# Output projection of a decoder layer: the sample rows multiply the raw fp32 weights in four column groups instead of split weights in a full-width tile

## The reference

```python
def _merge(x, attn, pool, ga, gb, ma, mb, gate, w_a_proj, w_b_proj, w_out):
    a = (attn * jax.nn.silu(ga)) @ w_a_proj
    bb = (pool * jax.nn.silu(gb)) @ w_b_proj
    m = jax.nn.sigmoid(ma) * a + jax.nn.sigmoid(mb) * bb
    return x + gate[:, None, :] * (m @ w_out)
```

## Time and profile before

| | us |
|---|---|
| median of 3 runs (lowest, highest) | 2156.23 (2155.46, 2157.18) |
| profiled execution, its own time | 2155.81 |
| span from the first to the last instruction | 2154.0 |
| TensorE matmuls busy in the span | 2027.2 (94%) |
| VectorE, GpSimd, ScalarE busy | 1252.5, 756.8, 493.6 |
| output projection | 1921.6 to the end |

### The profile page before, as it was taken

The page is one execution under the profiler, slowest core; times in us unless marked ns, Lnnn a source line. Parts: engine busy times, 40 slices in busy tenths (PEclk is TensorE's granted clock), DMA queues, the critical chain, the costliest instruction groups (busy, mean ns, idle before and its releaser), DMA issues.

```text
span 2154.0 us, 35342 instructions
## 1 busy us (share of the span) xinstructions
PE 2027.2 (94%) x15138; PEld 1850.8 (86%) x15138; DVE 1252.5 (58%) x1510; ACT 493.6 (23%) x621; POOL 756.8 (35%) x254
## 2 busy tenths in 40 slices
PE   4699999998999999999999999999988899989997
PEld 1289999988898988898999999999877898877776
DVE  2356666576787878885556777779533721133223
ACT  3222222342212222222112211112211311122222
POOL 0043333552233323233333444444444343323331
PEclk7799999999999999999999999999999999999999
DMA  9942223534232322233332233333466564633222
GB/s 343 353 141 79 78 79 92 156 105 140 71 83 68 82 74 78 72 87 107 80 98 70 69 97 99 96 97 105 136 171 167 167 196 142 201 111 125 86 100 102
DMA packets 325058, 258.68 MB, mean 120 GB/s; under 512 B 6587, under 2 KB 275063, under 8 KB 323655
## 3 DMA queue, kind: packets, MB, share of 16 engines
q1 hardware_dynamic: 312943, 228.10, 36.1%
q0 software_dynamic: 5120, 16.77, 2.6%
q10 hardware_dynamic: 6912, 12.59, 1.9%
HBM read 246.43 MB, written 11.48 MB: 120 GB/s over the span
## 4 chain that ended last, share of the span: by engine, by line
PE 79%; DVE 11%; DMA 5%; issue 2%; ACT 1%; SPq 0%; POOL 0%; DVEq 0%; ACTq 0%; POOLq 0%
PE acc L1358 59%; PE ps L1746 8%; DMA ring<-in_w_ada 4%; DVE ebuf L1060 2%; DVE qiT L935 2%; PE ps L1426 1%; PE acc L1746 1%; DVE ebuf L1061 1%; PE ps L1542 1%; PE ps L1552 1%; DVE idx L1056 1%; DVE scoreS L1058 1%; PE ps L1532 1%; PE ps L1683 1%; DVE misc L1053 1%
## 5 line engine op out<-in xcount | busy, mean ns | idle before, releaser
L463 POOL TENSOR_TENSOR wlo<-raw,whi 128x2048 fp32r<-128x2048 f32 (+1 forms) x170 | 681.8, 4015 | 1085.0 <-ACT whi L560 1084.6
L1358 PE MATMUL acc<-act_hi,whi 128*128 128x260 f32 x3904 | 814.3, 290 | 11.3 <-DVE act_lo L1188 6.2
L1358 PE MATMUL acc<-act_hi,wlo 128*128 128x260 f32 x3904 | 788.2, 283 | 0.0
L1358 PE MATMUL acc<-act_lo,whi 128*128 128x260 f32 x3904 | 787.6, 283 | 0.0
L1358 PEld LDWEIGHTS acc<-act_hi,whi 128*128 128x128 f32 x3904 | 607.7, 190 | 48.7 <-issue 38.3
L1358 PEld LDWEIGHTS acc<-act_lo,whi 128*128 128x128 f32 x3904 | 604.7, 189 | 0.0
L1358 PEld LDWEIGHTS acc<-act_hi,wlo 128*128 128x128 f32 x3904 | 604.1, 189 | 0.0
L560 ACT CAST whi<-raw 128x2048 fp32r<-128x2048 f32 (+1 forms) x154 | 280.9, 1824 | 1046.5 <-PE acc L1358 876.2
L935 DVE TENSOR_TENSOR qiT<-qiT,swp 128x520 f32<-128x520 f32 x32 | 142.7, 4461 | 1.1
L1746 PE MATMUL ps<-whi,act_hi 128*128 128x512 f32 x256 | 102.7, 401 | 7.7 <-DVE act_lo L1258 7.7
L1241 DVE TENSOR_TENSOR big<-acc,big 128x520 f32<-128x520 f32 x16 | 11.2, 699 | 164.2 <-PE acc L1358 164.2
(11 more groups left out here) (276 smaller groups left out, 2156.6 us busy)
## 6 DMA issues: line engine op xcount, KB each, us to landing
raw<-in_w_in SPq DMA_DIRECT2D x106, 1024.0 KB, 5.7
ring<-in_w_ada SPq DMA_DIRECT2D x32, 1024.0 KB, 14.2
raw<-in_w_a_proj SPq DMA_DIRECT2D x16, 1024.0 KB, 6.9
gate_unit<-in_w_ada SPq DMA_DIRECT2D x16, 1024.0 KB, 5.7
raw<-in_w_out SPq DMA_DIRECT2D x16, 1024.0 KB, 5.1
raw<-in_w_b_proj SPq DMA_DIRECT2D x16, 512.0 KB, 5.1
x_tok<-in_x_prompt SPq DMA_DIRECT2D x4, 1024.0 KB, 16.6
att_dram<-silu_ga ACTq DMA_DIRECT2D x16, 256.0 KB, 3.2
```

The costliest lines, as they stand in the source:

```text
L463: return nc.gpsimd.tensor_tensor(wlo[p][:, a:b], raw[p][:, a:b], whi[p][:, a:b].bitcast(F32), ALU.subtract)
L1358: last = mm(acc[p][:, a, 0:HALF], w, x[:, k, a * HALF:(a + 1) * HALF], start=(k == 0 and n == 0), stop=(k == kt - 1 and n == 2))
```

## The change

The sample tile no longer uses split operands. `sm` becomes an unsplit fp32 tile of 32 columns per k-tile (8 used, 24 zero), filled by one VectorE copy ahead of the `act_lo` series. In each quarter the four k-tiles go to four groups of 32 output rows of `acc[0]`, each one fp32 product of `sm` with the raw weights. At the end of a chunk all 128 rows are copied to `srow`, and one fp32 product with the existing table `sum4` adds the four groups. `sel8` and its load go. Since `raw` is now read by TensorE, each later load waits for `sample_used`; the load loop over the chunks is written out. Chunk 0 takes the tiles in the order 0, 4, 1, 2, 3, with the selection product behind tile 1 of its last quarter. The loads of gates, `g_final` and `x` additionally wait for `m_split`.

```diff
-    sm = at("sm", Z, [P, KT, P], F32R)
+    sm = at("sm", Z, [P, KT, 32])
-    srow = at("srow", A0 + 2816, [2 * NB, 512])
+    srow = at("srow", A0 + 2816, [P, 512])
-    sel8 = misc[0:16, 414:478]
-                         (sel8, t["k_sel"]),
@@ SyncE
         for kq in range(2, 4):
+            sp.wait_ge(S("sample_used"), kq - 1)
             load(Q_G + 1, kq - 2, quarter(w_out, kq, 0))
         sp.wait_ge(S("sm_ready"), 1)
+        sp.wait_ge(S("m_split"), KT)
         sp.wait_ge(S("gate_stored"), 4 * 16)
...
-        with sp.Fori(1, 4) as c:
+        for c in range(1, 4):
             for kq in range(4):
+                sp.wait_ge(S("sample_used"), 4 * c + kq - 1)
                 load(Q_G + 2 * c + kq // 2, kq % 2, quarter(w_out, kq, 512 * c))
@@ ScalarE
-        act.wait_ge(S("sm_zero"), 1)
-        nc.scalar.copy(sm[:, :, 0:NB], big2[:, :, SEQ:TOK]).then_inc(S("sm_hi_ready"), 1)
...
-            order = (0, 1, 2, 3, 4) if first else (0, 4, 1, 2, 3)
-            for n, i in enumerate(order):
+            for n, i in enumerate((0, 4, 1, 2, 3)):
@@ VectorE
-        v.memset(sm[:].bitcast(F32), 0.0).then_inc(S("sm_zero"), 1)
+        v.memset(sm[:], 0.0).then_inc(S("sm_zero"), 1)
         v.memset(ssq[:], 0.0).then_inc(S("sm_zero"), 1)
+        dve.wait_ge(S("sm_zero"), 1)
+        dve.wait_ge(S("m_ready"), KT)
+        v.tensor_copy(sm[:, :, 0:NB], big2[:, :, SEQ:TOK]).then_inc(S("sm_ready"), 1)
         for k in range(KT):
             dve.wait_ge(S("m_hi_ready"), k + 1)
...
-        dve.wait_ge(S("sm_hi_ready"), 1)
-        v.tensor_tensor(sm[:, :, NB:2 * NB], big2[:, :, SEQ:TOK], sm[:, :, 0:NB].bitcast(F32), ALU.subtract
-                        ).then_inc(S("sm_ready"), 1)
...
-        def sample_halves(c, done, count):
-            dve.wait_ge(done, count)
-            v.tensor_copy(srow[:], acc[0][0:16, 0, :]).then_inc(S("srow_ready"), 1)
+        def sample_halves(c):
+            dve.wait_ge(S("sample_used"), 4 * c + 4)
+            v.tensor_copy(srow[:], acc[0][:, 0, :]).then_inc(S("srow_ready"), 1)
...
-        for i in range(4):
-            out_rows(0, i, S("y_mm"), i + 1)
-        sample_halves(0, unit_done[1], Q_G + 2)
+        out_rows(0, 0, S("y_mm"), 1)
+        sample_halves(0)
+        out_rows(0, 1, S("y_mm"), 2)
         sample_rows(0)
-        times_g(0, (0, 1, 2, 3, 4))
+        out_rows(0, 2, S("y_mm"), 3)
+        out_rows(0, 3, unit_done[1], Q_G + 2)
+        times_g(0, (0, 4, 1, 2, 3))
@@ TensorE
-            mm(acc[0][0:64, 1, :], sel8, srow[:], start=True, stop=True).then_inc(S("srow_mm"), 1)
+            mm(acc[0][0:NB + 1, 1, :], sum4, srow[:], start=True, stop=True).then_inc(S("srow_mm"), 1)
...
-            order = (0, 1, 2, 3, 4) if first else (4, 0, 1, 2, 3)
+            order = (0, 4, 1, 2, 3) if first else (4, 0, 1, 2, 3)
...
+                if first and i == 4 and kq == 0:
+                    pe.wait_ge(S("sm_ready"), 1)
                 for kk in range(4):
                     k = 4 * kq + kk
+                    if i == 4:
+                        last = mm(acc[0][32 * kk:32 * kk + 32, 0, :], sm[:, k, :], raw[p][:, kk * 512:(kk + 1) * 512],
+                                  start=(kq == 0), stop=(kq == 3))
+                        continue
...
-                        trio = ((sm[:, k, :], wh), (sm[:, k, :], wl))
-                        o = acc[0][:, 0, :]
...
+                if i == 4:
+                    last.then_inc(S("sample_used"), 1)
+                if kq == 3 and i != order[-1]:
+                    if i < 4:
+                        last.then_inc(S("y_mm"), 1)
+                    if i == (1 if first else 0):
                         sample_sum(c)
...
-            if first:
-                sample_sum(c)
```

More of the change, by code:

```diff
@@ L566, in root @@
                                  scale=1.0 / D).then_inc(S("root_ready"), 1)
-        act.wait_ge(S("tables_landed"), 12 * 16)
+        act.wait_ge(S("tables_landed"), 11 * 16)
         nc.scalar.copy(identb[:], ident[:]).then_inc(S("identb_ready"), 1)
@@ L850, in _ @@
         dve.wait_ge(S("pages_landed"), 16)
-        dve.wait_ge(S("tables_landed"), 12 * 16)
+        dve.wait_ge(S("tables_landed"), 11 * 16)
         for i in range(4):
@@ L1312, in final_rows @@
         def final_rows(i):
-            out_rows(3, i, *((S("y_mm"), 14 + i) if i < 3 else (unit_done[1], Q_END)))
+            out_rows(3, i, *((S("y_mm"), 10 + i) if i < 3 else (unit_done[1], Q_END)))
         def later_rows(c, final=False):
             dve.wait_ge(S("xch_landed"), 16 * (c + 1))
-            sample_halves(c, S("y_mm"), 4 * c + 1)
-            out_rows(c, 0, S("y_mm"), 4 * c + 2)
+            sample_halves(c)
+            out_rows(c, 0, S("y_mm"), 3 * c + 1)
             sample_rows(c)
@@ L1323, in later_rows @@
             else:
-                out_rows(c, 1, S("y_mm"), 4 * c + 3)
-                out_rows(c, 2, S("y_mm"), 4 * c + 4)
+                out_rows(c, 1, S("y_mm"), 3 * c + 2)
+                out_rows(c, 2, S("y_mm"), 3 * c + 3)
                 out_rows(c, 3, unit_done[1], Q_G + 2 * c + 2)
@@ L1375, in _ @@
         tr = nc.tensor.transpose
-        pe.wait_ge(S("tables_landed"), 12 * 16)
+        pe.wait_ge(S("tables_landed"), 11 * 16)
         tr(ps[:, 0, 0:128], rows_cs[:], ident[:])
@@ L1730, in out_chunk @@
                         pe.wait_ge(S("attS_ready"), NB)
+                if first and i == 4 and kq == 0:
+                    pe.wait_ge(S("sm_ready"), 1)
                 for kk in range(4):
                     k = 4 * kq + kk
+                    if i == 4:
+                        last = mm(acc[0][32 * kk:32 * kk + 32, 0, :], sm[:, k, :], raw[p][:, kk * 512:(kk + 1) * 512],
+                                  start=(kq == 0), stop=(kq == 3))
+                        continue
                     if first and i == 0:
                         pe.wait_ge(S("m_split"), k + 1)
-                    if first and i == 4 and k == 0:
-                        pe.wait_ge(S("sm_ready"), 1)
                     wh, wl = (w[p][:, kk * 512:(kk + 1) * 512] for w in (whi, wlo))
-                    if i < 4:
[L1739 to L1742, removed]
-                        trio = ((sm[:, k, :], wh), (sm[:, k, :], wl))
-                        o = acc[0][:, 0, :]
[L1745 to L1749, removed]
+                    s = slice(i * P, (i + 1) * P)
+                    trio = ((act_hi[:, k, s], wh), (act_hi[:, k, s], wl), (act_lo[:, k, s], wh))
+                    for n, (x, w) in enumerate(trio):
+                        last = mm(ps[:, i, :], x, w, start=(k == 0 and n == 0), stop=(k == KT - 1 and n == 2))
+                if i == 4:
+                    last.then_inc(S("sample_used"), 1)
+                if kq == 3 and i != order[-1]:
+                    if i < 4:
+                        last.then_inc(S("y_mm"), 1)
+                    if i == (1 if first else 0):
                         sample_sum(c)
@@ L1778, in shape_constants @@
     cos, sin = np.cos(ang).astype(np.float32), np.sin(ang).astype(np.float32)
-    sel = np.zeros((16, 64), np.float32)
-    for r in range(16):
-        sel[r, r % 8] = 1.0
     cnt = np.stack([np.minimum(np.arange(16) + 1, w) for w in WINDOWS]).astype(np.float32)
@@ L1784, in shape_constants @@
         "k_cos": np.concatenate([cos, cos]), "k_sin": np.concatenate([sin, -sin]),
-        "k_ident": np.eye(P, dtype=np.float32), "k_sel": sel,
+        "k_ident": np.eye(P, dtype=np.float32),
         "k_rcnt": np.ascontiguousarray(np.broadcast_to((1.0 / cnt).astype(np.float32).reshape(1, 64), (P, 64))),
```

## The result

The changed kernel takes 2138.07 us (median of 4 runs, 2133.37 to 2141.01) beside 2155.85 us for the kernel before (4 runs); the ratio is 0.9913 with a 95% interval of 0.9898 to 0.9928. I had forecast 2142.8 us and a range of 2139.8 to 2147.0. The sign was right, the gain was 17.8 us where I had 13.4, and the median lies 1.7 us under the range. Later comparisons of the same kernel gave 0.9897 and 0.9911. The ratios and their intervals are those on record; they are not the quotients of the medians.

The account below looks back on a forecast made before the run. The prediction took TensorE to bound the output projection. Terms 10.7 - 0.1 + 1.4 + 1.3 - 0.1 + 0.2 = 13.4 us off 2155.81 gave 2142.4, and 0.4 for the median 2142.8 us; range 2139.8 to 2147.0.

Parts of the forecast that it names:

- What bounds the stage: Output projection: TensorE is busy nearly throughout, so time spared it after 1926.5 us shortens the kernel one for one.
- Sample products: Sample tile in each of 16 quarters: a block costs 1.19 us with edges instead of 1.86, saving 10.7 us.
- The first selection product: End of chunk 0: TensorE waits 1.0 us for `srow`, costing 2.1 us instead of 2.04; term -0.1 us.
- +0.8: First selection product: the term in us if VectorE's add of row 0 had not been held.
- Loads: Weight loads waiting for `sample_used`: 5.9 us of cover and more behind it in later chunks, so cost 0.
- last quarter: Chunk 3: 6.77 us pass before the fourth quarter needs its low part, ready at 6.70 plus a semaphore; -0.1 us.
- beginning of the kernel: SyncE's queue: one table load of 0.31 us gone ahead of the big weight loads; +0.2 us (0 to 0.3).
- Start of the stage: Start of output projection: earlier first `act_lo` spares six products, +1.4 us, and the clock returns sooner, +1.3 us.
- the cliff: Start of the stage: 0.04 us decided whether GpSimd's low part or the `act_lo` for k-tile 1 went first.
- my own range: Whole kernel: 2140.2 to 2145.0 us, from the start's bounds and an edge of 0.02 us per block; chance 0.68.
- clock term: Start of the stage: TensorE's clock back sooner, bounds 0 and 2.62 us, the middle taken, +1.3 us.

Follow-up runs that it names:

- e3_one_column_group: Changed kernel with the four sample products of a quarter all in one group of 32 output rows; 2178.48 us, ratio 1.0083 to the kernel before.
- e7_after_late_loads: Changed kernel with each later weight load released at the end of the quarter that read its buffer; 2145.16 us, ratio 0.9945 to the kernel before.
- e2_after_big_clear: Changed kernel with a further clear of 128 x 1536 unread values ahead of the `act_lo` series; 2145.26 us, ratio 0.9936 to the kernel before.
- e5_before_start_only: Kernel before, split products kept, with clears, copy into `sm`, subtraction and the gate, `g_final` and `x` loads moved; 2146.35 us, ratio 0.9952 to the kernel before.
- e8_after_again: Changed kernel measured again, unaltered, beside other variants on the same chip; 2134.65 us, ratio 0.9897 to the kernel before.
- e9_after_with_table: Changed kernel with the dropped `sel8` table load put back, read by nobody; 2137.64 us, ratio 0.9916 to the kernel before.
- e12_before_again: Kernel before measured against itself as a control; 2156.06 us, ratio 1.0005.
- e1_before_late_clear: Kernel before with the clears of `sm` and `ssq` moved behind the 16 `act_lo`; 2157.38 us, ratio 1.0 to the kernel before.
- e11_after_third: Changed kernel measured a third time, unaltered; 2136.81 us, ratio 0.9911 to the kernel before.

## Why the prediction was wrong, step by step

**What bounds the stage.** Right. TensorE waits in the changed stage for 3.0 us at its start and 1.1 us for `srow`, and for nothing else. The four terms below add up to the gain of the stage: 10.7 - 0.3 + 6.4 + 0 = 16.8 us.

**Sample products, 10.7 us.** Right. Quarters of 12.36 instead of 13.03 us, 0.67 each, 10.7 in 16. Of the Trainium skill I had weighed two places. "TensorE: Matmul & The Clock Gate", "Part 3: Packing small matmuls — row/col tiling", gives 2.38 times for three groups, and my estimate from it was 3.2 times for four; e3_one_column_group measures 3.55 in this shape, 1.00 against 3.55 us. What the drain at a change of tiling mode costs ("TensorEngine Tiling (Array Packing)", "Key Properties") can be no more than the edges, 0.1 us each, which the timeline after shows again.

**The first selection product, -0.1.** Right by its mechanism: the add of row 0 takes 3.58 us beside GpSimd, `srow` is copied behind it, TensorE waits 1.1 us (forecast 1.0). From the sample block ahead (1948.22 + 11.36) to the next one (1965.69 + 5.79) are 11.90 us; less 1.00 for the block and 8.57 for 36 products with their edges, the selection product costs 2.3 us where I had 2.1, so the term is -0.3. In e7_after_late_loads, where the add is not held, the wait is gone, which is the +0.8 that I had put beside it.

**Loads, last quarter, beginning of the kernel.** Their cost was 0 or too small to see. e7_after_late_loads shows that the cover holds in regular quarters and that I had not looked at the one quarter where it is thin; a release 11 us later cost 4.9 us of standing there, and 1.6 of clock behind it. The last quarter shows no loss (forecast -0.1).

**Start of the stage, 1.4 + 1.3 = 2.7 us. This is the step that failed.** The first quarter, from the last product ahead to its own last, takes 24.2 us before and 17.1 after (1914.96 to 1932.0, the end of 36 of the 48 products from 1923.50). Less the 0.67 of the product that is 6.4 us where I had 2.7. Most of the 3.7 us between is the wait: TensorE stood for 4.38 and 3.27 us before and for 3.03 after, which is 4.6 us where I had 1.4; what is left, 1.8 us, is nearly all the clock, where I had 1.3 (low-clock products cost some 3.2 us more than at full clock before, 1.5 after).

I wrote that "k-tiles 1 and 2 are through and k-tile 3 is the held one". None of the four that the first 12 products need was held. My first `act_lo` was due 2.66 us after the last product, and it came at 2.17. Of the 0.49 us, 0.32 are a gap that stood ahead of the long clear (1918.70 to 1919.07, "0.38 <-issue" in the earlier trace rows) and that I carried over; ahead of the short clear it is 0.06. The rest is my allowance for waits. With 2.17 the fourth `act_lo` started 0.11 us before GpSimd; with 2.66 it would have started some 0.4 after, and that decides whether VectorE stands for 4.5 us ahead of a product that TensorE wants next.

I had seen the cliff (0.04 us decided the order before), and still gave it bounds from 0 to 1.4 + 2.62, as if the better side ended at "three through". One k-tile more was not in the range. That this start costs so much is shown from both sides: e2_after_big_clear puts most of it back into the changed kernel and loses 7 to 8.5 us of stage, e5_before_start_only takes it out of the kernel before and gains 8.7. The fast end of my own range, 2140.2, was also not what its bounds give: 2142.8 - 1.3 - 0.3 is 2141.2.

The clock was the smaller part. It fell in the changed kernel too, but only for a part of the first 12 products. Busy time by stretch, columns as in the earlier trace rows:

```profile
1919.00:1919.50 0.50, 0.50 (x3) 0.40 (x2) 0.50 (x2) 0.50 (x2) 0.43 (x1) 0.61 0.00 0
...
1922.50:1923.00 0.50, 0.50 (x8) 0.09 (x8) 0.50 (x1) 0.50 (x2) 0.50 (x1) 0.97 0.00 0
```

The 12 products took 4.50 us there and 3.01 us in e8_after_again, where the clock stays at 1.00 and the stage is 1.5 us shorter (207.0). So the clock term was 1.8 us in the first profile and would be 3.3 in that one, above my upper bound of 2.62, which left out the three products ahead of the second stop. The same kernel gives both: in the seven profiles in which TensorE had stood for 3.03 us the clock fell in four (the 12 products took 4.25 to 4.50 us) and held in three (3.01). After 2.23 us of standing it held in all four profiles; after 4.38 and 4.64 us it fell within the first three products in all three. What decides it at 3.03 us no run shows.

**What stays open.** The medians differ by 17.8 us at first and by 18.5 and 22.3 later; over all 13 runs of the changed kernel (2136.8) and 50 of the kernel before (2156.5) it is 19.8. The stage explains 16.8 to 18.7. The 1 to 3 us above lie ahead of it, where the beginning of the stage scatters from 1909.2 to 1920.5 us over fourteen profiles of kernels that are the same there but for a table load (and, in three, two clears just ahead). The five profiles with the table load begin the stage at 1917.2 to 1920.5, mean 1919.2; the nine without it at 1909.2 to 1920.1, mean 1915.6. That points at the table, for which I had 0.2 us, and the times of e9_after_with_table are too wide to say yes or no. Whether the rest is scatter or a gain of a few microseconds from the missing load stays open.

## What to carry to other kernels

Where one engine's series of short operations races another engine's long one, work out which operation of the series starts last before it, from distances that count from the same event, and give the forecast both sides of each such edge: here less than half a microsecond decided 4.5 us of standing. Clear scratch tiles where their engine is idle, not at the head of a stage. And take a change apart before crediting its idea: 8.7 us were to be had in the old kernel by moving two clears, a copy and a subtraction.

## What the runs showed of the hardware that I had not expected

Four fp32 products of 32 columns and a 512-column stream take 1.00 us in four column groups and 3.55 us in one.
A VectorE `act_lo` subtraction that is already running when GpSimd's `wlo` subtraction begins is not stopped; GpSimd's takes longer instead, the more the longer they overlap: 4.54 us with 0.12 us of overlap (before), 4.77 with 0.37 (e2_after_big_clear), 5.03 with 0.58 (after). One that starts 0.04 us after GpSimd's is held to its end (5.07 us, before and e12_before_again).
Ahead of a VectorE clear there is a gap of 0.38 us when it clears 2048 columns (in two places, and e1_before_late_clear), 0.27 us for 1536 and 0.06 us for 512. I know no reason.
The granted clock after 3.03 us of standing differs between executions of one kernel: it fell to 0.50 in e11_after_third and stayed at 1.00 in e8_after_again.
